# Next round's gate products move from the second doubling level of a recurrent mixer to its state section, and to another PSUM bank

## The reference, cut to what matters

```python
r, k, v, xw, xa, xg = split_cols(p, RWKV_SPLITS)
w = -jax.nn.softplus(-(w0 + jnp.tanh(xw) @ w_decay_up)) - 0.5
decay = jnp.exp(-jnp.exp(w.astype(f32)))
a = jax.nn.sigmoid(a0 + xa @ a_up)
g = jax.nn.sigmoid(xg) @ g_up                  # the gate: 160 -> 1024
...
def step(state, inp):
    r_t, w_t, k_t, v_t, kk_t, a_t = inp
    sa = jnp.einsum('bhvk,bhk->bhv', state, -kk_t)
    state = (state * w_t[:, :, None, :] + sa[..., None] * (kk_t * a_t)[:, :, None, :]
             + v_t[..., None] * k_t[:, :, None, :])
    return state, jnp.einsum('bhvk,bhk->bhv', state, r_t)
...
return ((yn + bonus) * g.astype(f32)).astype(p.dtype)
```

## Time and profile before

| what | value |
|---|---|
| median of 3 runs | 2650.77 us |
| lowest and highest | 2650.51 and 2651.02 us |
| span of the profiled execution, first to last instruction | 2650.5 us |
| PE busy | 2622.0 us, 99% of the span |
| DVE busy | 1931.6 us, 73% |
| ACT busy | 1381.8 us, 52% |
| mean granted clock of PE | 0.999 |

### The profile page before, as it was taken

One profiled execution on the slowest core, in us unless ns is written; L12 is line 12 of the kernel. 1 busy time (PEld: TensorE's weight loads), 2 busy tenths in 40 slices (PEclk: granted clock), 3 DMA queues, 4 the chain that ended last, 5 costly groups with the idle time before them and its releaser, 6 DMA issues.

```text
span 2650.5 us, 46085 instructions
## 1 busy us (share of the span) xinstructions
PE 2622.0 (99%) x16930; PEld 2259.3 (85%) x16930; DVE 1931.6 (73%) x2963; ACT 1381.8 (52%) x2153; POOL 148.1 (6%) x162
## 2 busy tenths in 40 slices
PE   9999999999999999999999999999999999999998
PEld 8888888889888888888888888888888888888886
DVE  6778676877877877878887666578877756775676
ACT  6545555676544534435554454345455535553554
POOL 5600002301000000000000000000000000000000
PEclk9999999999999999999999999999999999999999
DMA  7555103555787787878778855677665555555554
GB/s 262 174 192 175 58 4 129 181 186 215 266 300 280 285 296 278 295 281 283 278 274 304 292 177 184 203 275 281 247 206 188 194 192 189 189 194 191 188 193 151
DMA packets 159504, 578.42 MB, mean 218 GB/s; under 512 B 18224, under 2 KB 18768, under 8 KB 158288
## 3 DMA queue, kind: packets, MB, share of 16 engines
q1 hardware_dynamic: 156224, 563.59, 61.3%
q10 hardware_dynamic: 2080, 9.46, 1.0%
q0 software_dynamic: 1008, 2.71, 0.4%
HBM read 572.81 MB, written 2.11 MB: 217 GB/s over the span
## 4 chain that ended last, share of the span: by engine, by line
PE 95%; DVE 2%; issue 1%; ACT 1%; POOL 1%; DMA 0%; SPq 0%; ACTq 0%; DVEq 0%; POOLq 0%
PE ps L2742 34%; PE ps L2746 18%; PE ps L2824 12%; PE ps L2826 12%; PE ps L2825 12%; PE ps L1151 1%; PE ps L1802 1%; PE ps L1164 0%; POOL ssm L1900 0%; DMA raw<-in_stream 0%; DVE wlo L2282 0%; PE ps L1100 0%; PE ps L2808 0%; PE ps L2809 0%; PE ps L2807 0%
## 5 line engine op out<-in xcount | busy, mean ns | idle before, releaser
L2282 DVE TENSOR_TENSOR wlo<-raw,whi 128x1024 fp32r<-128x1024 f32 x872 | 1059.3, 1230 | 516.8 <-ACT whi L1933 514.1
L1933 ACT ACTIVATE whi<-raw 128x1024 fp32r<-128x1024 f32 x871 | 903.3, 1056 | 778.7 <-PE ps L2746 367.9
L2742 PE MATMUL ps<-xn,whi 128*128 128x512 f32 x3760 | 941.3, 392 | 2.7 <-DVE wi L618 1.0
L2742 PEld LDWEIGHTS ps<-xn,whi 128*128 128x128 f32 x3760 | 674.7, 188 | 123.4 <-issue 2.2
L2746 PEld LDWEIGHTS ps<-xn,wlo 128*128 128x128 f32 x3760 | 510.8, 191 | 37.4 <-DVE wlo L2282 0.4
L2746 PE MATMUL ps<-xn,wlo 128*128 128x256 f32 x3760 | 520.6, 282 | 0.0
L2824 PE MATMUL ps<-whi,act_in 128*128 128x512 f32 x1120 | 436.1, 389 | 0.0
L2826 PE MATMUL ps<-whi,act_in 128*128 128x512 f32 x1120 | 435.7, 389 | 0.0
L2825 PE MATMUL ps<-wlo,act_in 128*128 128x512 f32 x1120 | 435.7, 389 | 0.0
L2824 PEld LDWEIGHTS ps<-whi,act_in 128*128 128x128 f32 x1120 | 210.2, 188 | 44.7 <-DVE wlo L2282 1.0
L2826 PEld LDWEIGHTS ps<-whi,act_in 128*128 128x128 f32 x1120 | 210.2, 188 | 43.7
(11 more groups left out here) (344 smaller groups left out, 2233.0 us busy)
## 6 DMA issues: line engine op xcount, KB each, us to landing
raw<-in_stream SPq DMA_DIRECT2D x872, 512.0 KB, 4.2
adaw<-in_ada SPq DMA_DIRECT2D x96, 512.0 KB, 5.8
adaq<-in_ada SPq DMA_DIRECT2D x96, 512.0 KB, 5.0
h<-in_xT SPq DMA_DIRECT2D x8, 256.0 KB, 8.9
memx<-in_memT ACTq DMA_DIRECT2D x1, 2048.0 KB, 9.2
gate_row<-gates POOLq DMA_DIRECT2D x2, 1024.0 KB, 7.6
lwa<-in_lora ACTq DMA_DIRECT2D x2, 512.0 KB, 4.5
lwa<-in_lora ACTq DMA_DIRECT2D x1, 1024.0 KB, 8.6
```

Source lines behind the costliest of these rows:

```text
L1933: act.activation(whi[:, r, :], raw[:, r, :], ACT.Copy).then_inc(hi_done, 1)
L2282: dve.tensor_tensor(wlo[:, r, :], raw[:, r, :], whi[:, r, :].bitcast(F32), ALU.subtract)\
L2742: return pe.matmul(ps[:, lin.bank(g, t), :], whi[:, (p0 + s) % RING, c * 512 + t * P:c * 512 + (t + 1) * P], x[:, 2 * s + c, :], start=s + ...
```

## The change

The gate products of round i+1 are no longer issued between product and doubled of level 2. Each lane's two matmuls stand right behind that lane's first state product, and go to bank 4g in place of 4g+2 (columns 256 to 511 as before). The wait ahead of them is now on `n2` of their lane, the wait that the state product ahead of them has as well. ACT's two gate copies move from level 2, where they stood between the sigmoids and the key gains, to behind `y1`, ahead of the table load. `spread_k_t` loses its wait on the gate copy; the outputs "yy", which write the same bank, get one. The first round's gates, which are made earlier beside the input projection, stay as they were.

```diff
-    PA = steps("prep_a", "kq gg root sg aa am e1 e2 ta tb tc", "kq root sg aa gg am e1 e2 ta tb tc")
-    PT = steps("prep_t", "kn wa g rb bs tr")
+    PA = steps("prep_a", "kq gg root sg aa am e1 e2 ta tb tc", "kq root sg aa am e1 e2 gg ta tb tc")
+    PT = steps("prep_t", "kn wa g rb bs tr", "kn wa rb bs g tr")
...
-             dict(kn=lambda g: 4 * g + 2, wa=lambda g: 4 * g + 3, g=lambda g: 4 * g + 2, rb=lambda g: 4 * g + 2,
+             dict(kn=lambda g: 4 * g + 2, wa=lambda g: 4 * g + 3, g=lambda g: 4 * g, rb=lambda g: 4 * g + 2,
...
                 sigmoids_a(act, i + 1)
-                gate_a(act, i + 1)
                 key_gain_a(act, i + 1)
...
             applied(i)
-            if not more:
+            if more:
+                gate_a(act, i + 1)
+            else:
                 exponentials(5)
             preload(act, ACT.Sqrt)
...
-    def gate_t(pe, i):
-        for g in lanes:
+    def gate_t(pe, i, which=lanes):
+        for g in which:
             n = 2 * i + g
             if i:
-                PD.wait(pe, g, i, "km")
+                CD.wait(pe, g, i - 1, "n2")
...
     def spread_k_t(pe, i):
             PD.wait(pe, g, i, "kv")
-            if i:
-                PA.wait(pe, g, i, "gg")
...
                     CT.done(ins, g, f"s{c}")
+                    if i < 3 and c == 1:
+                        gate_t(pe, i + 1, (g,))
             for g in lanes:
                 if i == 3 and g == 0:
                     unused(2, 4)
+                if i < 3:
+                    PA.wait(pe, g, i + 1, "gg")
                 CD.wait(pe, g, i, "s3")
...
             product(i, 2)
-            if more:
-                gate_t(pe, i + 1)
             doubled(i, 2)
```

## The result

The changed kernel takes 2664.76 us (median of 5, 2662.0 to 2667.5) against 2650.82 (median of 5, 2650.51 to 2651.56): a ratio of 1.005 [1.004, 1.0061] (here and below, the 95% interval in brackets), slower by 0.5% or 13.9 us. The forecast was 2651.5 with no difference that can be told. The profiled execution took 2665.15 us with a span of 2663.4, against the span of 2650.5 before.

What follows compares the result with a forecast made beforehand. PE was taken to bound the kernel, holding 95% of the chain. Rounds 0 and 1 (+1.50) and round 2 (-0.75) gave +0.75 on the span of 2650.5, and 0.27 more for the median: 2651.5 us, range 2649.5 to 2654.9.

Steps and rivals of the forecast that it cites:

- The gain in level 2: Product 3 starts 0.45 us earlier per round, 1.35 over three, bound by DVE's scans; a PE hole of 1.49 remains.
- The copies on ACT: Moving ACT's two gate copies, 0.70 us, out of level 2 gains 0, since PE does not wait for ACT there.
- The state section: Gate products there delay the outputs by 1.20 us per round in rounds 0 and 1.
- Round 2: In its state section the gate fills PE's wait of 1.08, the clock stays up, and outputs come 0.30 us earlier.
- rival 5: PE's pause for "issue" in round 2 goes, 0.45 us less, 2651.1; chance 0.63 together with the main sum.
- The clock against the new holes: Level 2's new 1.49 us holes leave PE's clock up, cost 0; one fall was priced at 1.08 us.
- Rival 2: The holes in level 2 lower the clock in one to three rounds: 2652.6 to 2654.8 us; chance 0.15.
- my sum: All three rounds together: +1.50 for rounds 0 and 1, -0.75 for round 2, so +0.75 us.
- Rival 3: Clock falls in level 2 and again in the state section, every round: up to +10.2 us, 2661.0; chance 0.04.
- The base: Whole kernel: a span of 2650.5 us before, with the median taken as 0.27 above the span.

Runs made afterwards that it cites:

- hole_only: Kernel before without the later rounds' gate products and copies, leaving the hole in level 2 alone: 2666.78 us, ratio 1.0044.
- dense_behind: Changed kernel with five unused wide products behind product 3, so the hole ahead of it stays: 2662.67 us, ratio 1.0043.
- fill_dense: Changed kernel with five unused products of 128 columns in the hole of level 2: 2653.42 us, ratio 1.0005.
- fill_half: Changed kernel with two unused wide products in the hole of level 2: 2653.29 us, ratio 1.0006.
- scans_behind: Changed kernel with DVE's two scans moved behind its copies of level 2: 2651.59 us, ratio 1.0007.
- split: Kernel before with only lane 0's gate moved to the state section, lane 1's left in level 2: 2651.34 us, ratio 1.0003.
- state_only: Kernel before with an unused second set of gate products in the state section, level 2 as before: 2654.66 us, ratio 1.0012.
- split_turn: As split, with the last third of lane 0's turning also moved behind the second state products: 2651.66 us, ratio 0.9999 against the kernel before.
- fill_small: Changed kernel with twenty small unused products, shaped like the level's own, in the hole of level 2: 2656.62 us, ratio 1.0025.

## Why the prediction was wrong

*The gain in level 2, "0.45 us per round":* right in mechanism, 0.57 in size. The scans bound the level, product 3 came when they ended, and a hole was left (1.34 for a forecast 1.49). The idle time printed ahead of DVE's copy was not the whole gain, since the copy then started 0.08 before the end of the scans' row (306.71 + 1.42 against 308.05).

*The copies on ACT, 0:* right. No wait of PE from a round's first state product to its outputs ends at ACT, and the table load stayed under cover.

*The state section, "1.20 us per round":* right, 1.21 and 1.23.

*Round 2, "-0.30":* right, and the granted clock there was 1.00. That its pause for "issue" could go (rival 5) was wrong: it grew from 0.45 to 0.92.

*"The clock against the new holes ... I take 0":* this is the step that failed, in its chance and in its size. I trusted a row of a single execution: at 440 to 442 PE was idle for 2 us at a granted clock of 1.00, and I took this as a reason that a hole of 1.49 would pass. In the changed kernel's profiled execution the clock fell behind that very wait of 2.13 us. The same wait stands in the profiled executions of all twelve kernels of this case, and in eight of them the clock fell behind it, for 3.4 us each. `hole_only` shows the same from the other side: ten executions with the same holes had mean clocks from 0.998 down to 0.989. One row says that a fall need not follow, not that it will not.

The size was 1.08, the turning's share of a fall in the state section that lasted 3.4 us (393.3 to 396.8). A fall behind the hole of level 2 lasted 13.7 us and cost 5.34 and 5.4. The price went with how long the clock stayed low, at 0.4 to 0.5 us for each us: 1.4 for 3.4 us in round 0 of `dense_behind` and 1.42 for 3.4 at the mixer's end, 5.4 for 13.7 here, 6.5 (20.23 - 13.77) for 17.1 in `hole_only`. I had taken the length from another stretch.

*The rivals.* Rival 2, the holes lower the clock, is what happened, in two rounds of three in the profiled execution; its 2652.6 to 2654.8 is 10 us short for want of that price. With the measured one, my sum would have been +0.75 - 3 x 0.12 + 5.34 + 5.41 = +11.1; the pause (+0.47) and the mixer's end (+1.42) make it 13.0. Rival 3 came nearest, 2661.0, but by luck: 6.2 of its 10.2 us are falls in the state sections, and there was none.

*The base.* I added 0.27 us between span and median, from two different executions. In each execution listed with both, the time is 1.7 to 1.9 us above the span, so by an estimate the profiled execution of the kernel before took about 2652.3, some 1.5 more than the median. That does not move the forecast of the median (2650.77 + 0.75 = 2651.5), but it is why the spans differ by 12.9 us and the medians by 13.9.

What the runs show: the hole in level 2 is what lowers the clock in the rounds (`fill_dense`, `fill_half`, `scans_behind` and `split` shorten or remove it, `hole_only` has it alone, `state_only` does not have it). What stays open: why round 1 of the changed kernel's profiled execution escaped, with the same hole of 1.34 us and the same product ahead of it; and whether the small dummies failed in three executions for their shape or for the short idle time left ahead of product 3 (up to 0.18 us in the profiled execution, which had no fall). On PE, rounds 1 and 2 are alike up to the hole (4.33 us from product 1 to product 2 and 3.51 to product 3 in both), and only round 2 fell.

## What to carry to other kernels

Work that stands in front of a wait for another engine may be what keeps PE's clock up: before it is moved away, price the hole that it leaves as a possible fall to half clock, over all of the PE-bound stretch behind the hole and not over the hole. Where such a hole must stay, unused products of 128 columns in it cost no time here (3.50 us for the level with and without) and removed nearly all of the loss. And a single row in which the clock stayed up is no evidence that it always does: look for the same kind of wait elsewhere in the trace, and give the fall a chance of its own.

## What the runs showed of the hardware that was not expected

- Busy time alone did not bring the clock back. In the changed kernel PE was busy without a gap from 310.2 to 323.9 us at 0.50, through products of levels 3 to 5 and the helper products between them; it rose near the end of the first products of `applied` (L1176). In round 2 it rose among the same products, at about 399.
- The fall can begin inside the hole (`hole_only`, at about 306.6, the hole lying from 306.1 to 307.4) or 1.8 us after its end (the changed kernel, 310.2).
- The pause of PE put down to "issue" ahead of the state section of round 2 changes with the program: 0.45 us before, 0.92 after the change, 1.11 and 1.13 in `split` and `split_turn`, 1.24 in `fill_small` (and 0.61 in its round 1). It does not simply grow with the number of instructions ahead of it: `fill_half` and `fill_dense` add products to the changed kernel and have 0.19 and none. What causes it was not tried.
